# Gate chunks of 32 instead of 64 tokens, and the first up parts between the down products, in a PEER block kernel

## What is computed

```python
q = (xt @ w_query).reshape(T, PEER_HEADS, 2, D_HALF)
s = jnp.einsum('thpd,hpnd->thpn', q, sub_keys)
...                                   # top 16 of each half, then top 16 of the sums
ids = (i1 * N_KEYS + i2).reshape(T, PEER_HEADS * PEER_TOPK)
gates = jax.nn.softmax(best_s, axis=-1)
a = jnp.einsum('tkd,td->tk', expert_down[idb], xb)
act = jax.nn.gelu(a, approximate=False) * gb
y = jnp.einsum('tk,tkd->td', act, expert_up[idb])
```

## Time and profile before

| | us |
|---|---|
| median of 3 runs | 1520.45 (1516.05 to 1521.91) |
| profiled execution | 1526.2 |
| its span | 1524.4 |
| PE busy | 1457.1 |
| DVE busy | 1164.4 |
| ACT busy | 626.3 |
| POOL busy | 587.1 |

### The profile page before, as it was taken

One profiled execution on the slowest core, in us unless ns is written; L12 is line 12 of the kernel. 1 busy time (PEld: TensorE's weight loads), 2 busy tenths in 40 slices (PEclk: granted clock), 3 DMA queues, 4 the chain that ended last, 5 costly groups with the idle time before them and its releaser, 6 DMA issues.

```text
span 1524.4 us, 21239 instructions
## 1 busy us (share of the span) xinstructions
PE 1457.1 (96%) x7494; PEld 1255.7 (82%) x7494; DVE 1164.4 (76%) x2434; ACT 626.3 (41%) x985; POOL 587.1 (39%) x460
## 2 busy tenths in 40 slices
PE   3999999999999989999979999999999999999997
PEld 3455548999999889999978888888888888888886
DVE  6557465567888978888737878778778888888887
ACT  3134433344544457676633333333333333333333
POOL 0000011136444357999904333344334434434340
PEclk8999999999999999999989999999999999999999
DMA  9944304447464355776699999998989999999993
GB/s 355 387 162 166 97 28 132 131 134 239 145 197 159 124 190 216 269 253 243 246 373 356 356 341 348 361 362 313 381 306 356 351 360 344 335 383 349 332 329 114
DMA packets 161113, 404.88 MB, mean 266 GB/s; under 512 B 12968, under 2 KB 76016, under 8 KB 159984
## 3 DMA queue, kind: packets, MB, share of 16 engines
q1 hardware_dynamic: 122320, 243.87, 44.8%
q0 software_dynamic: 36864, 134.23, 24.4%
q10 hardware_dynamic: 1824, 25.43, 4.2%
HBM read 360.49 MB, written 42.99 MB: 265 GB/s over the span
## 4 chain that ended last, share of the span: by engine, by line
PE 52%; POOL 6%; issue 2%; DMA 2%; DVE 1%; ACT 0%; SPq 0%; POOLq 0%; ACTq 0%; DVEq 0%
PE bank L1815 11%; PE bank L1816 11%; PE bank L1817 11%; PE bank L1742 5%; PE bank L1744 5%; PE bank L1743 5%; POOL gated L725 5%; PE bank L1797 2%; POOL own L722 1%; DMA down<-in_down_t 1%; POOL rows L678 1%; DMA gate<-gates_dram 1%; DVE yn L1523 0%; DVE x L1504 0%; DVE dlo L1251 0%
## 5 line engine op out<-in xcount | busy, mean ns | idle before, releaser
L1742 PE MATMUL bank<-h2hi,dhi 128*128 128x384 f32 x1024 | 350.2, 342 | 16.7 <-DVE dlo L1251 16.7
L1744 PE MATMUL bank<-h2hi,dlo 128*128 128x384 f32 x1024 | 345.7, 338 | 0.0
L1743 PE MATMUL bank<-h2lo,dhi 128*128 128x384 f32 x1024 | 345.5, 337 | 0.0
L1251 DVE TENSOR_TENSOR dlo<-down,dhi 128x1024 fp32r<-128x1024 f32 x128 | 165.0, 1289 | 188.8 <-ACT dhi L858 186.0
L1815 PE MATMUL bank<-uhi,ahi 128*128 128x512 f32 x768 | 299.6, 390 | 4.0 <-DVE ulo L1478 4.0
L1816 PE MATMUL bank<-ulo,ahi 128*128 128x512 f32 x768 | 299.4, 390 | 0.0
L1817 PE MATMUL bank<-uhi,alo 128*128 128x512 f32 x768 | 299.2, 390 | 0.0
L678 POOL DMA_INDIRECT rows<-in_peer_up,ids x128 | 162.7, 1271 | 238.4 <-DVE y L1328 207.1
L678 POOL DMA_INDIRECT rows<-in_peer_down,ids x128 | 159.6, 1247 | 224.0 <-DVE rows L1319 187.6
L1742 PEld LDWEIGHTS bank<-h2hi,dhi 128*128 128x128 f32 x1024 | 194.5, 190 | 22.1 <-DVE dlo L1251 19.2
L1743 PEld LDWEIGHTS bank<-h2lo,dhi 128*128 128x128 f32 x1024 | 194.7, 190 | 2.8 <-issue 0.2
(11 more groups left out here) (201 smaller groups left out, 1950.3 us busy)
## 6 DMA issues: line engine op xcount, KB each, us to landing
down<-in_down_t SPq DMA_DIRECT2D x128, 512.0 KB
up<-in_peer_up SPq DMA_DIRECT2D x128, 512.0 KB
ada<-in_w_ada SPq DMA_DIRECT2D x48, 512.0 KB, 11.0
gate<-gates_dram SPq DMA_DIRECT2D x32, 768.0 KB
gates_dram<-stage ACTq DMA_DIRECT2D x5, 4096.0 KB
gel_dram<-gel SPq DMA_DIRECT2D x80, 192.0 KB
gelu<-gel_dram SPq DMA_DIRECT2D x80, 192.0 KB
wq<-in_peer_query SPq DMA_DIRECT2D x16, 512.0 KB, 4.3
```

The source lines that it names most:

```text
L1251: ve.tensor_tensor(dlo[s][:], down_tile(n)[:], dhi[s][:].bitcast(F32), ALU.subtract).then_inc(dve_dlo, 1)
L1742: pe.matmul(bank[7 * s][:, 0:TD], dhi[s][:, k, :], h2hi[:, k, 0:TD], start=k == 0, stop=False)
L1743: pe.matmul(bank[7 * s][:, 0:TD], dhi[s][:, k, :], h2lo[:, k, 0:TD], start=False, stop=False)
L1744: last = pe.matmul(bank[7 * s][:, 0:TD], dlo[s][:, k, :], h2hi[:, k, 0:TD], start=False, stop=k == KT - 1)
```

## The change

The chunk is 32 tokens, so there are twelve chunks of two turns, and the stage buffers are 16 KB each. Each holds two gate buffers and one yn later on. The 32 KB set free hold up0, uhi1, uhi2, ulo1, ulo2, two row buffers and junk; before that, during the search, its first part holds search buffers and the three row buffers of the heads. up0 is loaded together with up1 and up2, after the row operations of the search. POOL's waits for the gate stores are gone. On ACT `uhi` of up tiles 0 and 1 is made between the gelus of tiles 76 to 79, on DVE `ulo` of both between the low parts of tiles 78 to 80; what follows them in the order before, `ahi` and `alo`, stays where it was. All other DMAs are of the same sizes; gate loads have runs of 4 x 32 values.

```diff
-CHUNK_T = 64
+CHUNK_T = 32
...
+        spare_at = r.at
+        spare_end = spare_at + 8 * D * 4
+        assert rows_heads_end <= spare_end
+        r = Region(nc, spare_end, limit)
...
+        gate, yn = [[], []], []
+        for k in range(2):
+            r = Region(nc, stage_at + k * KEYS * CHUNK_T * 4, stage_at + (k + 1) * KEYS * CHUNK_T * 4)
+            for g in range(2):
+                gate[g].append(r(f"gate{g}_{k}", [CHUNKS, GSET, CHUNK_T]))
+            yn.append(r(f"yn{k}", [D]))
+        r = Region(nc, spare_at, spare_end)
+        up = [r("up0", [D])] + up
...
             sp.wait_ge(act_pick, 3)
-            for u in range(1, SLOTS):
+            sp.wait_ge(dve_row, DOTS_ROUTING)
+            for u in range(SLOTS):
                 load_up(u)
...
             sp.wait_ge(stored[0], 16 * (CHUNKS // 2))
-            load_up(0)
             sp.wait_ge(act_g, TD // 4)
...
-            gp.wait_ge(stored[0], 16 * (CHUNKS // 2))
-            for n in range(asked, ROW_OPS):
-                if n == DOTS_EARLY + ROWS_KEPT:
-                    gp.wait_ge(stored[1], 16 * (CHUNKS // 2 - 1))
-                    gp.wait_ge(stored_part[0], 32)
-                    gp.wait_ge(stored_part[1], 32)
-                gather(n)
+            gathers(ROW_OPS)
...
             for n in range(AFTER_G, EARLY):
                 early(n, n % 2)
-            act.wait_ge(stored[0], 16 * (CHUNKS // 2))
+                if n - AFTER_G < AHEAD:
+                    up_hi(n - AFTER_G)
             for u in range(AHEAD):
-                parts_hi(u)
+                act_hi(u)
...
-            for n in range(AFTER_G, EARLY):
+            for n in range(AFTER_G, EARLY + 2):
                 down_lo(n, n % 2)
-            for n in range(EARLY, EARLY + 2):
-                down_lo(n, n % 2)
+                if 2 <= n - AFTER_G < 2 + AHEAD:
+                    up_lo(n - AFTER_G - 2)
             for u in range(AHEAD):
                 activations(u)
             for u in range(AHEAD):
-                parts_lo(u)
+                act_lo(u)
```

More of the change, by code:

```diff
@@ L355, in build_block @@
         stage = [r(f"stage{i}", [KEYS, CHUNK_T]) for i in range(2)]
-        assert rows_heads_end <= r.at
+        spare_at = r.at
+        spare_end = spare_at + 8 * D * 4
+        assert rows_heads_end <= spare_end
+        r = Region(nc, spare_end, limit)
         rows = [r(f"rows{i}", [D]) for i in range(ROWS_KEPT)] + rows_heads
@@ L371, in build_block @@
         gelu = [r(f"gelu{i}", [TD]) for i in range(2)] + [gelu2]
-        r = Region(nc, stage_at, stage_at + KEYS * CHUNK_T * 4)
+        gate, yn = [[], []], []
[6 more added lines that the diff above has]
+        up = [r("up0", [D])] + up
         uhi += [r(f"uhi{i}", [D], F32R) for i in range(1, SLOTS)]
         ulo += [r(f"ulo{i}", [D], F32R) for i in range(1, SLOTS)]
[L375 to L379, removed]
         rows += [r(f"rows{i}", [D]) for i in range(ROWS_KEPT + ROWS_HEADS, ROWS)]
-        yn = [r(f"yn{i}", [D]) for i in range(2)]
         junk = r("junk", [D])
@@ L1022, in _, with act_hi @@
                     early(FIRST_G + t, t % 2)
-            def parts_hi(u):
+            def act_hi(u):
                 j = u % SLOTS
@@ L1030, in parts_hi, with up_hi @@
                 act.activation(ahi[j][:], gelu[j][:], ACT.Copy).then_inc(act_ahi, 1)
+            def up_hi(u):
+                j = u % SLOTS
+                if u >= SLOTS:
+                    act.wait_ge(pe_u, u - SLOTS + 1)
                 act.wait_ge(up_in[j], 16 * (u // SLOTS + 1))
                 act.activation(uhi[j][:], up[j][:], ACT.Copy).then_inc(act_uhi, 1)
+            def parts_hi(u):
+                act_hi(u)
+                up_hi(u)
             def fused_gelu(n):
@@ L1471, in activations, with act_lo @@
                                  gate[g][k % 2][:, :, UPS[u] % GSET, :], ALU.mult).then_inc(dve_act, 1)
-            def parts_lo(u):
+            def act_lo(u):
                 j = u % SLOTS
@@ L1476, in parts_lo, with up_lo @@
                 ve.tensor_tensor(alo[j][:], gelu[j][:], ahi[j][:].bitcast(F32), ALU.subtract).then_inc(dve_alo, 1)
+            def up_lo(u):
+                j = u % SLOTS
                 ve.wait_ge(act_uhi, u + 1)
                 ve.tensor_tensor(ulo[j][:], up[j][:], uhi[j][:].bitcast(F32), ALU.subtract).then_inc(dve_ulo, 1)
-            for n in range(AFTER_G, EARLY):
+            def parts_lo(u):
+                act_lo(u)
+                up_lo(u)
+            for n in range(AFTER_G, EARLY + 2):
                 down_lo(n, n % 2)
-            for n in range(EARLY, EARLY + 2):
-                down_lo(n, n % 2)
+                if 2 <= n - AFTER_G < 2 + AHEAD:
+                    up_lo(n - AFTER_G - 2)
             for u in range(AHEAD):
```

## The result

The changed kernel takes 1511.19 us in the median of 11 runs (1507.19 to 1514.42), the kernel before 1517.99 beside it (1515.04 to 1521.91). The medians differ by 6.8 us (0.45%). The ratio on record, which is not the quotient of the medians, is 0.9944, with an interval of 0.9934 to 0.9955: 0.56% or 8.5 us, between 6.8 and 10.0. The forecast was 8.6 us. The profiled execution of the changed kernel has a span of 1511.8 us and lasted 1513.6.

The account below looks back on a forecast made before the run. PE was taken to bound the kernel, with a hole at the join before the long stretch. Earlier start 8.1, packets -0.3, clock 0.8 sum to 8.6 us: 1520.45 - 8.6 = 1511.85 us, range 1507 to 1519.

Parts of the forecast that it names:

- The bound and the size of the join: PE bounds the kernel, busy 700.00 of 700 us in the long stretch; the join can give 13.1 us at most.
- hole of 13.1 us: Between gate stage and long stretch: PE idle 5.25 and 4.14 us, plus 2.06 and 1.67 lost to slow clock.
- Start of product 0: At the join, up product 0 starts at 786.7, 8.1 us sooner, plus 0.3 for small packets.
- The landing of down load 79: At the join, with half the store in front, it should land near 772 to 774; before it took 14.25 us.
- The gathers: Gathers 35 and 36 go out near 762, ahead of down loads 79 and 80; 1.05 MB moves in both versions.
- The smaller store: Before the gate load, 2.10 MB of store and 0.52 of up0 are gone: 6.5 us earlier landing.
- The first up parts: Without uhi and ulo, 2.05 us instead of 3.6 remain from gate load landing to up product 0.
- The gate loads' packets: Runs of 512 B cost a few ns per packet: hidden in the long stretch, 0.3 us at the join.
- The rival of a DMA-bound stretch: Dear 512 B packets draw out the long stretch by 18 us: 1530. Chance 0.05.
- The half open hole: Gathers and small runs delay the join's gate load 3 to 4 us; gain about 5: 1515.5. Chance 0.28.
- The closed hole: Gate load lands in under 5 us, PE goes straight into product 0: 12.9 us, 1507.5. Chance 0.13.
- Stores that hold ACT: In the gate stage, stores hold ACT 0.5 to 1 us each, 10 times, eating the gain: 1520. Chance 0.05.

Follow-up runs that it names:

- e0_after: The changed kernel run again, beside the kernel before: ratio 0.9949, median 1511.84 us against 1519.24.
- e11: The changed kernel run once more on another chip, beside the kernel before: ratio 0.9952, median 1510.99 us against 1519.21.
- e3: Only the changed kernel's chunk size and memory; gathers 35 and 36, up0 and first up parts where they were before: ratio 0.9992, median 1517.72 us.
- e2: The changed kernel, but uhi and ulo of the first two up tiles again made behind the gated values: ratio 0.9965, median 1515.08 us.
- e8: The changed kernel, but for tiles 75 to 78 SP asks for the next down load before waiting for the gelu to store: ratio 0.9940, 1508.45 us.
- e9: The changed kernel with SP asking for down loads earlier at the join and chunks of 16 tokens: ratio 0.9935, median 1509.20 us.
- e4: The changed kernel with chunks of 16 tokens, gate loads in runs of 256 B: ratio 0.9953, median 1513.81 us.
- e5: The changed kernel, but 1.57 MB of the last store asked for only after the high part of down tile 79: ratio 0.9961, median 1516.19 us.
- e6: The changed kernel, but the store of the chunk before the last asked for with the last one's, 4.19 MB: ratio 0.9971, median 1518.13 us.
- e1: The changed kernel, but gathers 35 and 36 wait again for the stores of the gates: ratio 0.9970, median 1514.25 us.
- e10: The kernel before, chunks of 64, with SP asking for the next down load before the gelu wait for tiles 75 to 78: ratio 0.9998, 1518.66 us.
- e7_before: The kernel before, unchanged, one more profiled execution: 1520.8 us, span 1518.9.

## Why the prediction was right, point by point

**The bound and the size of the join** held. The long stretch stayed full, and the hole of 13.1 us (10.9 in the other profile) is where the gain came from; the differences of the times follow the holes. A forecast gain of 8.6 leaves 4.5 of the 13.1, and the mean of the three profiles after is 4.5, though its make-up was another than forecast.

**Start of product 0.** Forecast were 787.0, which is 28.5 us after the last gate product; the three profiles have 30.6, 27.6 and 29.8. The gate loads were to be asked for 18.2 us after it and were at 21.1, 18.5 and 20.3; the first landed in 7.28 us in e0_after, where 784.7 - 776.7 = 8.0 were implied. The landing of down load 79 was mis-sized: it should have come 8 to 10 us after its request and needed 12.63 and 11.92 in two of three profiles (10.1 in the third). And the mechanism failed there: the prediction takes the gate load alone to set product 0, and calls any start of tile 79 before 778.4 (19.9 us after the last gate product) good enough. Tile 79 started 20.1 and 19.4 us after it in after and e11, and the sum leaves out that the clock falls behind such a wait, which costs tiles 79 and 80 another 1.7 us (forecast: no clock of 0.50 there). In these two the chain goes from load 79 through tile 79 to product 0, with no wait for the gate load. Only e0 went as forecast: its gate load landed 25.8 us after the last gate product, where 26.2 were forecast.

**The gathers were put at 0, and that step failed.** "Before the gate load lands they have to move in both versions" counts bytes only. The gathers held back share the engines with the gate load itself (9.36 against 7.28 us): holding them back costs 2.4 us. They went out 2.9 and 4.1 us after the last gate product, near what 762 us stood for.

**The smaller store** was priced together with up0 by its bytes, 6.5 us of landing. Alone it gave 1.5 us or nothing, with the other parts 3 to 5, of which a part is ACT's time; and e3 leaves some 0.3 for up0. No run shows 6.5 us of landing for these bytes. That the sum of 8.6 came close all the same is luck: the gathers, which were not in it, made up for this.

**The first up parts** were put at 1.6 us; e2 shows 1.7 of order, and 1.7 of clock, of which the forecast had taken half.

**The gate loads' packets.** The price of a few ns was right: 4.5 to 6.6 ns each, 22 thousand in the long stretch, 6 to 9 us of engine time, and no PE wait. The estimate of 5 us by the Trainium skill (DMA: Bandwidth & Descriptors, section Why small descriptors are slow) is near the lower of these. The 0.0445 ns a byte are a little high for rows 7, which give 0.0432 and 0.0437; nothing hangs on it. The rival of a DMA-bound stretch is out, even at 256 B.

**The rivals.** The half open hole is in part what happened: holes of 5.7 and 5.0 us stay in two of three profiles, and the gain of 6.8 by the medians lies between its 5 and my 8.6, that by the ratio (8.5) at my number. The closed hole needed one more step, SP's order (e8, e9). Stores that hold ACT were not seen: none of the waits in the gate stage is for `gates_dram`. What I overlooked was the base. I took the hole of the profile before for typical; it was 2.1 us larger than in the second profile. And 1520.45 was the median of three runs, that of eleven is 1517.99. The time of 1511.19 lies within 0.7 us of my 1511.85 because a base 2.5 us too high met a gain that is 1.8 us smaller by the medians: that nearness is luck as well.

## What to carry to other kernels

A transfer that is off the critical path still costs by what it runs beside: ask which load the next stage waits for, and keep other traffic away from it, rather than counting bytes up to a date. Where two waits follow each other, price both: here the one thought harmless was on the path in two profiles of three, because the clock fell behind it. Take the parts of a change out one at a time as well as putting one in: here the smaller store alone was worth 1.5 us at most in the medians and the whole 7. Take a second profile of the kernel before where a few us matter: one stage differed by 3.4 us between two executions of the same kernel.

## What the runs showed of the hardware

- SP's queue with packets down to 256 B: each further packet cost 4.5 ns (after) and 7.0 ns (e4), or 6.6 and 8.1 with the bytes made equal, from 57 to 124 thousand packets in 690 us.
- A gate load of 768 KB took 7.3 to 8.5 us with no gathers asked for beside it (e0, e2, e4, e5, e6, e8) and 9.4 and 10.0 us with two of 512 KB asked for in the 2.4 us before it (e1, e3; in e3 up0 too).
- A gate load requested 5.5 us earlier onto full queues (e10) landed only 1.2 us earlier: it took 14.17 instead of 9.86 us.
- The granted clock after an idle piece: PE was idle for 2.74 us ahead of product 0 in e7_before and in e2_late_parts alike; the clock stayed at 2.4 GHz in the first and fell to 1.2 in the second. Gaps of 2.03 us and less saw no fall, 2.75 (e11_after) and all longer ones did. So near 2.7 us the length of the gap alone does not say it. Windows of e7_before, then of e2_late_parts:

```profile
790.00:792.00 2.00, 1.12 (x5) 0.97 (x6) 2.00 (x3) 2.00 (x3) 0.00 (x0) 1.00 0.54 131
```

```profile
786.00:788.00 2.00, 2.00 (x6) 1.51 (x6) 2.00 (x3) 0.00 (x0) 0.77 (x1) 0.50 0.90 296
```
